# The second block's gate tiles as seven block products between the heads of its attentions

## What is computed

```python
h = rms_norm(x, attn_norm)
proj = h @ w_in
aq, ak, av, iq, ik, iw, bq, bk, bv, gates = split_cols(proj)   # gates: 2 * D_MODEL = 2048 columns
ya = sparse_attention(aq, ak, av, iq, ik, iw, k_sel)           # attention A, 8 heads
yb = diff_attention(bq, bk, bv, lam)                           # attention B, 4 heads of 2 components
g = sigmoid(gates + gate_bias)
g_a, g_b = split(g, 2)
merged = g_a * (ya @ w_up_a) + g_b * (yb @ w_up_b)
x = x + merged @ w_out
x = x + (silu(gate) * up) @ w_ffn_out                          # gate, up = split(rms_norm(x) @ w_ffn_in)
```

## Time and profile before

| | us |
|---|---|
| median of 3 runs (2799.04 to 2804.67) | 2803.46 |
| the profiled execution's own time | 2802.99 |
| its span | 2801.2 |
| TensorE busy | 2734.2 (98%) |
| VectorE busy | 1253.1 (45%) |
| ScalarE busy | 597.5 (21%) |
| GpSimd busy | 297.0 (11%) |
| granted clock of TensorE, mean | 0.988 |

### The profile page before, as it was taken

How to read it: one execution, slowest core, us unless ns; L and a number is a source line. 1 busy time by engine, 2 the same in 40 slices (tenths; PEclk the granted TensorE clock), 3 DMA queues, 4 the chain that set the end, 5 groups by cost and what they waited for, 6 DMA issues and landing times.

```text
span 2801.2 us, 55963 instructions
## 1 busy us (share of the span) xinstructions
PE 2734.2 (98%) x22540; PEld 1884.1 (67%) x22540; DVE 1253.1 (45%) x2618; ACT 597.5 (21%) x1291; POOL 297.0 (11%) x490
## 2 busy tenths in 40 slices
PE   7999999999999999999999999999999999999999
PEld 5887899988876332323222232268879998878999
DVE  4555589744253023233231314254534752642674
ACT  3334444332242000100000000014331002351000
POOL 4000000000000222122212222103100000300000
PEclk9999999999999999999999999999999999999999
DMA  9455578842223999999999999954434554434542
GB/s 292 155 177 166 168 250 274 270 123 70 88 80 141 358 375 371 386 383 374 375 367 379 364 386 369 356 165 130 127 120 151 167 165 126 134 119 137 163 161 98
DMA packets 460994, 634.49 MB, mean 227 GB/s; under 512 B 29850, under 2 KB 278832, under 8 KB 460608
## 3 DMA queue, kind: packets, MB, share of 16 engines
q1 hardware_dynamic: 456896, 626.14, 65.2%
q10 hardware_dynamic: 1440, 3.52, 0.3%
q0 software_dynamic: 2400, 1.26, 0.2%
HBM read 629.76 MB, written 1.05 MB: 225 GB/s over the span
## 4 chain that ended last, share of the span: by engine, by line
PE 71%; SPq 19%; issue 5%; DMA 3%; DVE 1%; ACT 1%; ACTq 0%; DVEq 0%
PE bank L568 48%; PE accum L568 22%; SPq L3163 12%; SPq L3158 3%; SPq L3144 2%; DMA ring<-in_moe_w_dram 2%; DMA ring<-in_ada_w_dram 1%; SPq L3073 1%; DVE w L2088 1%; PE bank L689 1%; DMA w<-in_moe_w_dram 0%; PE accum L955 0%; PE bank L1208 0%; ACT L1557 0%; ACT sh L1557 0%
## 5 line engine op out<-in xcount | busy, mean ns | idle before, releaser
L568 PE MATMUL bank<-h,ring 128*128 128x256 f32 (+2 forms) x2272 | 455.1, 361 | 2.4 <-ACT h L1557 2.0
L568 PE MATMUL bank<-w 64*64 64x64 f32 (+5 forms) x5394 | 427.0, 317 | 4.9 <-ACT w L1661 2.3
L568 PEld LDWEIGHTS bank<-h,ring 128*128 128x128 f32 (+1 forms) x2272 | 391.0, 191 | 56.3 <-issue 9.9
L568 PEld LDWEIGHTS bank<-w 64*64 64x64 f32 (+3 forms) x5394 | 288.6, 143 | 136.4 <-issue 127.1
L568 PE MATMUL bank<-w,ring 128*128 128x256 f32 (+1 forms) x1660 | 304.1, 339 | 0.9 <-ACT w L1674 0.9
L568 PEld LDWEIGHTS bank<-w,ring 128*128 128x128 f32 x1660 | 268.1, 191 | 27.2 <-ACT w L1674 1.4
L568 PE MATMUL accum<-w 128*128 128x128 f32 (+6 forms) x2192 | 264.7, 387 | 0.2
L568 PE MATMUL bank<-ring,w 128*32 (+1 forms) x1742 | 240.9, 592 | 0.0
L568 PEld LDWEIGHTS accum<-w 128*128 128x128 f32 (+3 forms) x2192 | 184.6, 164 | 58.5 <-issue 50.3
L568 PE MATMUL accum<-h,ring 128*128 128x256 f32 (+2 forms) x1184 | 222.0, 342 | 0.0
L2088 DVE TENSOR_TENSOR w<-accum,w 128x512 f32<-128x512 f32 x108 | 74.7, 692 | 285.6 <-PE accum L568 278.7
(11 more groups left out here) (351 smaller groups left out, 3125.5 us busy)
## 6 DMA issues: line engine op xcount, KB each, us to landing
ring<-in_moe_w_dram SPq DMA_DIRECT2D x816, 256.0 KB, 6.7
w<-in_moe_w_dram SPq DMA_DIRECT2D x528, 256.0 KB, 6.8
ring<-in_w_in_dram SPq DMA_DIRECT2D x76, 1024.0 KB, 5.3
ring<-in_ada_w_dram SPq DMA_DIRECT2D x48, 1024.0 KB, 5.9
ring<-in_w_ffn_in_dram SPq DMA_DIRECT2D x44, 1024.0 KB, 5.1
ring<-in_ffn_w_dram SPq DMA_DIRECT2D x30, 1024.0 KB, 7.7
ring<-in_w_ffn_out_dram SPq DMA_DIRECT2D x16, 1024.0 KB, 5.1
ring<-in_w_o_dram SPq DMA_DIRECT2D x8, 1024.0 KB, 5.0
```

The source lines that it names most:

```text
L568: ins = nc.tensor.matmul(o, lhsT, rhs, start=start, stop=stop, skip_group_check=skip)
```

## The change

The 16 gate tiles of a layer become eight units n = 0 to 7 of 256 columns, computed by the seven products. Where tile 2n stood in the table, part "a" of unit n stands now (four products); where tile 2n + 1 stood, part "b" (three products). Call them na and nb.

- GpSimd makes the four weight sums of each unit in two sets of buffers (`gate_weights`), the first as soon as its rotary copies are done. Set n % 2 is written again when unit n - 2's fourth sum has been used.
- VectorE makes the four token sums once per layer, behind the norm (`gate_tokens`). After each head's probabilities (`beside_b`, `beside_a`) it drains the parts into quarters (`gate_parts`): two adds per part.
- ScalarE copies the first product of "a" for VectorE (`gate_copies`), and when "b" has been drained puts the bias on the two finished tiles (`gate_biases`). Both now stand behind the head's copies (`behind`), no longer ahead of them.

Cut to its core:

```diff
 def gate_tiles(tag, hd):                                   # TensorE
     for m in GATES_AT[tag][hd + 1]:
+        n = m // 2
         if m % 2 == 0:
             held[:] = piece(8, 256)
         s, w = held
-        t, f = take(("gt", l, m))
-        lo = m % 2 * P
-        contract(t[:, 0:T], KD, lambda k: w(k, lo, lo + P), lambda k: h[:, k, :]).then_inc(f, 1)
-        if m % 2:
+        if m % 2 == 0:
+            t, f = take(("gt", l, n, "a"))
+            product(t[:, 0:P], lambda k: w(k, 0, P), B11, True)
+            product(t[:, P:2 * P], lambda k: w(half + k, 0, P), B21, False)
+            if n == 0:
+                pe.wait_ge(token_sums_ready, next_of("token_sums_ready"))
+            pe.wait_ge(gate_sums_ready, 8 * l + n + 1)
+            product(t[:, 2 * P:3 * P], S2, T2, False)
+            product(t[:, 3 * P:4 * P], S1, T1, False, f)
+        else:
+            t, f = take(("gt", l, n, "b"))
+            product(t[:, 0:P], S3, T3, True)
+            product(t[:, P:2 * P], S4, B22, False, gate_sums_used)
+            product(t[:, 2 * P:3 * P], lambda k: w(half + k, P, FW), T4, False, f)
             release.append(s)
...
-def gate_copies(tag, hd):                                  # ScalarE
-    for m in GATES_AT[tag][hd + 1]:
-        act.wait_ge(*full(("gt", l, m)))
-        fn(sg[:, m, :], psum_of(("gt", l, m))[:, 0:T], ACT.Identity, bias=col2(l, "gate_bias", m)
-           ).then_inc(reader_of(("gt", l, m)), 1)
+def gate_biases(ms):
+    for m in ms:
+        if m % 2:
+            act.wait_ge(*read_out(("gt", l, m // 2, "b")))
+            for i in range(2):
+                ins = fn(sg[:, m - 1 + i, :], gate_parts[m // 2 % 2][:, 2 * i:2 * i + 2, :], ACT.Identity,
+                         bias=col2(l, "gate_bias", m - 1 + i))
+            ins.then_inc(gate_biased, 1)
+def gate_copies(ms):
+    for m in ms:
+        if m % 2 == 0:
+            n = m // 2
+            act.wait_ge(*full(("gt", l, n, "a")))
+            if n > 1:
+                act.wait_ge(gate_biased, 8 * l + n - 1)
+            fn(gate_parts[n % 2][:, 7, :], psum_of(("gt", l, n, "a"))[:, 0:P], ACT.Copy).then_inc(gate_copied, 1)
+def behind_b(hd):
+    if hd:
+        gate_biases(GATES_AT["B"][hd - 1])
+    gate_copies(GATES_AT["B"][hd])
+def behind_a(hd):
+    gate_biases(GATES_AT["A"][hd - 1] if hd > 1 else GATES_AT["B"][4] if hd else GATES_AT["B"][3])
+    gate_copies(GATES_AT["A"][hd])
...
     elif hd == 9:                                          # in beside_a, behind head 7
-        for m in range(12, 16):
-            act.wait_ge(*read_out(("gt", l, m)))
+        gate_biases(GATES_AT["A"][7])
+        act.wait_ge(gate_biased, 8 * l + 8)
         for q in (2, 3, 0, 1):
...
+dve.wait_ge(h_ready, sent["h_ready"])                      # VectorE, once per layer
+token_sums(gate_tokens, h[:, :, :], KD // 2)
+def gate_quarters(ms):
+    for m in ms:
+        n, to = m // 2, gate_parts[m // 2 % 2]
+        if m % 2 == 0:
+            bank_a = psum_of(("gt", l, n, "a")).rearrange("p (i t) -> p i t", t=P)
+            dve.wait_ge(gate_copied, 8 * l + n + 1)
+            tt(to[:, 0:6:5, :], to[:, 7:8, :].to_broadcast([P, 2, P]), bank_a[:, 1:3, :], ADD).then_inc(dve_step, 1)
+            dve.wait_ge(dve_step, stepped())
+            tt(to[:, 4, :], to[:, 5, :], bank_a[:, 3, :], ADD).then_inc(reader_of(("gt", l, n, "a")), 1)
+        else:
+            ...
...
+for n in range(8):                                         # GpSimd, behind the layer's swaps
+    if n == 1:
+        pool.wait_ge(roped, sent["roped"] + l - 1)
+    if n > 1:
+        pool.wait_ge(gate_sums_used, 8 * l + n - 1)
+    pool.wait_ge(ring_loaded[s], 16 * uses)
+    pool.tensor_tensor(S1, A21, A22, ALU.add).then_inc(gate_added, 1)
+    pool.tensor_tensor(S3, A11, A21, ALU.subtract)
+    pool.wait_ge(gate_added, steps + 1)
+    pool.tensor_tensor(S2, S1, A11, ALU.subtract).then_inc(gate_added, 1)
+    pool.wait_ge(gate_added, steps + 2)
+    pool.tensor_tensor(S4, A12, S2, ALU.subtract).then_inc(gate_sums_ready, 1)
```

More of the change, by code:

```diff
@@ L531, in build, with four @@
         xg, sqg = tiles(18, 8), sg[:, 0:8, :]
+        def four(ap):
+            return [ap[:, 512 * i:512 * (i + 1)].rearrange("p (k t) -> p k t", t=P) for i in range(ap.shape[-1] // 512)]
+        gate_tokens = four(qa.rearrange("p j t -> p (j t)")) + four(up[:, 0, :])
+        gate_weights = [four(slot4(2, 2)), four(slot4(12)) + four(slot4(13)[:, 0:512]) + four(slot4(1)[:, 512:1024])]
+        gate_parts = [ap.rearrange("p (i t) -> p i t", t=P) for ap in (slot4(4), sh[:, 8:12, :].rearrange("p j t -> p (j t)"))]
         picked, placed, unpicked = words(16), words(16), words(16)
@@ L1459, in gate_tiles, with product @@
                 def gate_tiles(tag, hd):
+                    half = KD // 2
+                    B11, B12, B21, B22 = halves_of_tokens(h[:, :, :], half)
+                    T1, T2, T3, T4 = gate_tokens
+                    def product(o, left, right, opens, done=None):
+                        for k in range(half):
+                            ins = mm(o, left(k), right[:, k, :], opens and k == 0, k == half - 1,
+                                     last=done is not None and k == half - 1, skip=True)
+                        if done is not None:
+                            ins.then_inc(done, 1)
                     for m in GATES_AT[tag][hd + 1]:
+                        n = m // 2
                         if m % 2 == 0:
@@ L1629, in shift_h, with attention @@
                     fn(h[:, j, :], h[:, j, :], ACT.Identity, bias=shifts[:, j:j + 1]).then_inc(h_ready, one("h_ready"))
-            def attention(tag, beside=None):
+            def attention(tag, beside=None, behind=None):
                 sm, pb, pT, oT, mask, scale, n, comps = attention_plan(tag)
@@ L1648, in attention @@
                         weighted_sum(tag, hd - 2)
+                    if behind:
+                        behind(hd)
                 if beside:
@@ L2059, in _ @@
                     act.wait_ge(*read_out(("nat", l, 2 + n // 2, n % 2)))
-                attention(("B", l), beside_b)
+                attention(("B", l), None, behind_b)
                 act.wait_ge(*read_out(("B", l, "o", 2)))
@@ L2376, in gated @@
                             dve.wait_ge(dve_step, stepped())
-                            token_sums(hidden_sums_of(j), hidden[:, k0:k0 + 2 * half, :], half)
+                            token_sums([hidden_sums_of(j)[:, i] for i in range(4)], hidden[:, k0:k0 + 2 * half, :], half)
                 def finished(u):
@@ L2386, in finished @@
                         add_to_x(u - UP_UNITS, parts[u % 3])
-                token_sums(h_sums, h[:, :, :], KD // 2)
+                token_sums([h_sums[:, i] for i in range(4)], h[:, :, :], KD // 2)
                 first_sum(0)
@@ L3020, in beside_a @@
                         ins.then_inc(ysub, one("ysub"))
-                attention(("B", l), small[:, 8 + l:9 + l])
+                attention(("B", l), small[:, 8 + l:9 + l], beside_b)
                 attention(("A", l), None, beside_a)
@@ L3233, in _ @@
                         ins.then_inc(halves_swapped, one("halves_swapped"))
+                pool.wait_ge(halves_swapped, sent["halves_swapped"])
+                for n in range(8):
+                    s, uses = gate_at_slot[l, n]
+                    half = KD // 2
+                    w = ring[:, s, :].rearrange("p (k n) -> p k n", n=FW)
+                    A11, A12, A21, A22 = w[:, 0:half, 0:P], w[:, half:, 0:P], w[:, 0:half, P:FW], w[:, half:, P:FW]
+                    S1, S2, S3, S4 = gate_weights[n % 2]
+                    steps = 2 * (8 * l + n)
+                    if n == 1:
[9 more added lines that the diff above has]
+                    pool.tensor_tensor(S4, A12, S2, ALU.subtract).then_inc(gate_sums_ready, 1)
+                pool.wait_ge(gate_sums_ready, 8 * (l + 1))
         for (who, name), k in heard.items():
```

34 lines of the change are left out of this document (23 added, 11 removed).

## The result

The changed kernel takes **2812.42 us** (median of 6 runs, 2808.33 to 2815.49), the kernel before 2802.61 beside it (6 runs, 2799.04 to 2804.67). The ratio is 1.0037, 95% interval 1.0024 to 1.0050: slower by 9.8 us, outside the predicted range, where 2797.3 was forecast. The profiled execution took 2814.88 us, its span is 2812.4.

The account below looks back on a forecast made before the run. TensorE's work was taken as the bound, busy 78.87 of 80 us. 2802.99 - 10.5 (gate units) + 3.4 (first loss) + 1.4 (second loss) = 2797.3 us; range 2792.8 to 2803.5.

Parts of the forecast that it names:

- TensorE's part: Gate units: part "a" 3.58 us, "b" 2.68; each unit saves 0.66 us, 16 units 10.5 us.
- First loss, the roots: Attention A: TensorE stalls 2.1 us at head 2's weighted sum behind ScalarE's logs; 1.7 us lost per layer, 3.4 in all.
- Second loss, the sigmoids: Fourth up-projection tile: bias operations ahead of ScalarE's sigmoids stall TensorE 0.7 us per layer, 1.4 in all.
- VectorE: the step that failed: VectorE's token sums and drains, 1.55 us of drains per unit, fit its idle time and were costed at nothing.
- the two tight heads: Heads with little VectorE slack, head 2 of B tightest; drains slowed beside GpSimd cost at most 1.2 us in all.
- Head 2's slack of 0.6: Attention B: VectorE hands over head 2's probabilities after 5.6 us, TensorE wants them after 6.2; costed at nothing.
- GpSimd: right, and no comfort: Weight sums: 1.23 us per add, 4.9 per unit, covered because there was room for 2.1 us each.
- the reload: GpSimd's library reload before the first add, once in layer 0: room for 6.0 us, costed at nothing.
- The sum: Whole execution: 2802.99 us less TensorE's saving plus the two losses gives 2797.3 us.
- Rival 2: Thinner covers: late probabilities, 1.2 us, and a reload 1 to 4 us over its room; 2798.5 to 2802.5 us, 27%.
- Rival 3: GpSimd's sums become the bound, TensorE waiting before each unit's third product in B; 2812.5 us at 2.6 per add, 8%.

Follow-up runs that it names:

- e12: Changed kernel with adds in quarters for units 0 to 2, unit 3's whole adds behind head 2's probabilities, and e3's ScalarE order: 2794.64 us, ratio 0.9973.
- e9: Kernel before, with only e3's ScalarE order, no products or sums: 2799.69 us, ratio 0.9992.
- e3: Changed kernel with attention A's logs and roots, and the first eight tiles' sigmoids, moved later in ScalarE's order: 2806.40 us, ratio 1.0022.
- e1: Changed kernel with GpSimd's adds working on 8 elements per partition instead of 512: 2798.78 us, ratio 0.9989.
- e4: Changed kernel with 64 filler matmuls on TensorE ahead of its wait for head 0's probabilities in attention B: 2826.96 us, ratio 1.0096.
- e5: Changed kernel with unit 0 by the old contraction and GpSimd's sums for later units moved to where VectorE has slack: 2801.23 us, ratio 0.9994.
- e7: e5, but unit 0 keeps its products and its sums beside the selection, as in the changed kernel: 2806.07 us, ratio 1.0014.
- e8: Changed kernel with six of VectorE's one-operand SBUF operations taking every second element: 2813.05 us, ratio 1.0035.
- e10: Changed kernel with each GpSimd add of 128x512 issued as four of 128x128: 2799.26 us, ratio 0.9995.
- e11: Changed kernel with 18 filler matmuls, where e4 had 64, ahead of TensorE's wait for head 0's probabilities: 2809.60 us, ratio 1.0035.

## Why the prediction was wrong

**TensorE's part: right.** 3.57 and 2.68 us per unit, 10.5 us in all. Not all of it reaches the time even where the stalls are gone: e12's stages are 7.3 us shorter than e9's. The rest goes into short waits and gaps, 0.9 us per layer of them around unit 3.

**First loss, the roots: right.** Predicted 2.1 us stall at A's third weighted sum, measured 2.05 in both layers; from A's first scores (S) to that sum it is 2049.29 - 2027.16 = 22.1 us, where 22.2 was forecast. e3 removed it. What the step left out is that a stall of this length may be followed by a stretch at the lower clock: about 1.6 us behind seven of the 16 such stalls in the profiles of the changed kernel, e1, e4, e5, e7, e8, e10 and e11, none in the changed kernel's own.

**Second loss, the sigmoids: right.** Predicted 0.7 us, counted between starts; so counted it is 0.62 and 0.64, though the view of waits lists 0.36.

**VectorE: the step that failed.** It read: "The drains read PSUM as one operand; I cost that at nothing, with the upper end 0.3 us at the two tight heads of a layer". That was true of the drains and beside the point. The same paragraph had the row that mattered, VectorE's add at 0.98 instead of 0.69 us while GpSimd copies, and I asked only which *added* VectorE operations it would touch. It touches the *old* ones that run beside GpSimd's new adds: the last rotary add, six operations of the selection, and the normalising of head 0. I never looked at where VectorE stood when the adds would begin. Its slack there was visible before: 1.47 us at 1987.27, and at the probabilities some 1.8: head 0's last step was done by 1993.2, TensorE turned them at 1995.70, and the shorter unit takes 0.66 of that. e1 then showed 1.9. VectorE's last step of head 0, and TensorE's turn, before:

```profile
1992.51 0.75 DVE L2094 SCALAR_TENSOR_TENSOR w<-w,small 128x128 f32<-128x128 f32 x2
```

```profile
1995.70 0.55 PE L689 MATMUL bank<-con,w 128*128 128x128 f32 x3
```

Against this slack stood 0.95 us at the last rotary add (1.64 instead of 0.69), 4.8 in the selection and 2.4 up to the end of the normalising: 8.2 less 3.4 is the 4.81. Head 2's slack of 0.6 went the same way, 1.01.

**GpSimd: right, and no comfort.** An add takes 1.27 us where I took 1.23, TensorE never waited for a sum, and the reload cost nothing that the trace shows (last swap done at 1978.7, first add at 1978.80). The Trainium skill, "GPSIMD Engine Reference", section "Instruction dispatch", speaks of about 6 us there; no such gap exists in this trace. The rule of the Trainium skill on two-input work, in the same page's section "Engine selection", I weighed as GpSimd's own slowness alone; the price was paid by VectorE.

**The sum with the measured terms,** counted between starts: 2797.3 + 2 x (4.9 + 1.2) for the late probabilities, + 2.05 + 2.33 for the clock, - 2 x 0.2 for the two smaller losses = 2813.5 us. The profiled execution took 2814.9, the median is 2812.4. Rival 2 named the mechanism, late probabilities, but priced it at tenths per head; 16.6 us lay in it. Rival 3 looked for the danger in GpSimd's lateness, where it was in GpSimd's company; that one of its prices, 2812.5, equals the measured time is chance, since no such wait on GpSimd exists. The range failed since its upper end rested on that price of tenths, though the adds' effect on VectorE had been seen only beside copies.

Not settled: why some stalls of 2 us are followed by the slow stretch and others not, and what among operations with one operand in SBUF makes the tensor-scalar ones wait while maxima and reductions do not; no run here takes a tensor-scalar operation out of the two-port form.

## What to carry to other kernels

When work goes to GpSimd, ask not only whether it is done in time but what VectorE does on SBUF meanwhile and how much slack that has: each such operation can wait out one whole GpSimd instruction. Place GpSimd's work beside VectorE's reads of PSUM and its waits, or cut it into small instructions; cutting it won 12 us here although each sum then took 1.75 instead of 1.27 us. And compare stages of the traces, not only whole times. And count a wait of TensorE by its length and the stretch at half clock behind it.

## What was unexpected of the hardware

- Beside GpSimd's tensor-tensor adds (1.27 us) a VectorE operation of 0.35 us on SBUF takes up to 1.2 to 1.4 us, even one of 128x2 elements (1.27 instead of 0.17 us in e5). Maxima, match-replace, reductions and operations that read PSUM are not touched. GpSimd is held up too: 1.66 to 1.76 us.
- In quarters the same adds take 0.44 us each when alone, and VectorE's operations 0.36 to 0.6.
- A wait of 4.8 us was followed by 2.05 and 2.33 us lost to the clock in the two layers of the changed kernel; one of 2.05 us by about 1.6 us or by none.
